# Expert rows gathered in runs of four of one kind instead of in turns, in a one-core encoder layer

## The reference

```python
def _peer(u, w_query, sub_keys, expert_down, expert_up):     # u: 512 tokens x 1024
    ...
        qc = (xc @ w_query).reshape(PEER_CHUNK, PEER_HEADS, 2, PEER_DKEY // 2)
        s_half = jnp.einsum('chpk,pnk->chpn', qc, sub_keys, ...)
        top_s, top_i = lax.top_k(s_half, PEER_TOPK)            # 16 of 128, twice
        ...                                                    # best 16 of the 256 sums
        expert = jnp.take_along_axis(cand_i, best_j, axis=-1)  # of 16384 experts
        g = jax.nn.softmax(best_s, axis=-1)
        u_e = expert_down[expert]                              # one row of 1024 each
        act = jax.nn.gelu(jnp.einsum('chkd,cd->chk', u_e, xc, ...), approximate=False)
        v_e = expert_up[expert]
        return jnp.einsum('chk,chkd->cd', (g * act).astype(xc.dtype), v_e)
```

## Time and profile before

| | us |
|---|---|
| median of 3 runs (1945.47 to 1947.72) | 1947.72 |
| the profiled execution's own time | 1944.45 |
| its span, first to last instruction | 1942.6 |
| PE busy / DVE busy / POOL busy | 1549.1 / 1161.1 / 1002.8 |
| ACT busy | 399.5 |
| mean granted TensorE clock | 0.952 |

### The profile page before, as it was taken

The page is one execution under the profiler, slowest core; times in us unless marked ns, Lnnn a source line. Parts: engine busy times, 40 slices in busy tenths (PEclk is TensorE's granted clock), DMA queues, the critical chain, the costliest instruction groups (busy, mean ns, idle before and its releaser), DMA issues.

```text
span 1942.6 us, 14519 instructions
## 1 busy us (share of the span) xinstructions
PE 1549.1 (80%) x4216; PEld 706.7 (36%) x4216; DVE 1161.1 (60%) x2797; ACT 399.5 (21%) x984; POOL 1002.8 (52%) x1053
## 2 busy tenths in 40 slices
PE   5979999999688779698777879876787877767777
PEld 3434455656333234343223434322233322222223
DVE  6523057749666776576565766676665557666651
ACT  2100045512212212121211211221211211111111
POOL 3000000004566766766666666666666666666663
PEclk8889999999799999899999989999998999999989
DMA  9776242207999999999999999999999999999995
GB/s 321 241 258 194 79 130 44 78 32 229 404 357 374 390 386 366 393 409 370 388 400 350 373 389 407 366 378 367 365 370 373 383 363 351 375 378 377 360 375 226
DMA packets 192772, 620.26 MB, mean 319 GB/s; under 512 B 25695, under 2 KB 26103, under 8 KB 192535
## 3 DMA queue, kind: packets, MB, share of 16 engines
q0 software_dynamic: 147456, 536.94, 72.1%
q1 hardware_dynamic: 45238, 82.41, 12.9%
HBM read 613.12 MB, written 6.16 MB: 319 GB/s over the span
## 4 chain that ended last, share of the span: by engine, by line
PE 29%; POOL 23%; issue 14%; DVE 13%; DMA 12%; another core or an unknown queue 6%; ACT 1%; SPq 1%; DVEq 0%; POOLq 0%; ACTq 0%
POOL big L567 17%; PE pair L577 13%; PE pair L749 13%; POOL region_v L567 5%; DMA big<-in_expert_up,expert_idx 5%; DVE big L1228 4%; DMA big<-in_expert_down,expert_idx 4%; PE pair L613 1%; DMA region_v<-in_expert_up,expert_idx 1%; DMA big<-in_w_in 1%; DMA big<-in_w_ada 1%; DVE region_v L1228 1%; PE pair L701 1%; DVE big L1081 1%
## 5 line engine op out<-in xcount | busy, mean ns | idle before, releaser
L749 PE MATMUL pair<-big 128*128 128x512 f32 x1544 | 764.1, 622 | 206.2 <-DMA big<-in_expert_up,expert_idx 107.1
L1228 DVE CUSTOM_DVE_ANT_0 big<-big,pair 128x1024 f32<-128x1024 f32 x378 | 459.6, 1220 | 304.6 <-DMA big<-in_expert_down,expert_idx 219.7
L749 PEld LDWEIGHTS pair<-big 128*128 128x128 f32 x1544 | 276.0, 194 | 613.1 <-issue 581.9
L567 POOL DMA_INDIRECT big<-in_expert_up,expert_idx x386 | 365.9, 948 | 243.4 <-issue 102.1
L567 POOL DMA_INDIRECT big<-in_expert_down,expert_idx x378 | 360.3, 953 | 118.3 <-issue 108.6
L749 PE MATMUL pair<-region_v,big 128*128 128x512 f32 x504 | 258.3, 636 | 67.2 <-DMA region_v<-in_expert_up,expert_idx 39.1
L577 PE MATMUL pair<-big 128*128 128x512 f32 (+1 forms) x656 | 288.3, 617 | 20.1 <-DMA big<-in_w_in 14.0
L1228 DVE CUSTOM_DVE_ANT_0 region_v<-region_v,pair 128x1024 f32<-128x1024 f32 x134 | 162.9, 1220 | 96.8 <-DMA region_v<-in_expert_down,expert_idx 67.8
L894 ACT ACTIVATE big<-ident,big 128x128 f32<-128x128 f32 x512 | 157.9, 388 | 271.4 <-issue 126.2
L533 POOL TENSOR_SCALAR small<-small 128x4 f32<-128x4 f32 x5 | 1.2, 232 | 356.4 <-DVE small L1106 337.9
L567 POOL DMA_INDIRECT region_v<-in_expert_down,expert_idx x134 | 130.1, 971 | 101.3 <-DVE expert_idx L1166 49.4
(11 more groups left out here) (140 smaller groups left out, 966.0 us busy)
## 6 DMA issues: line engine op xcount, KB each, us to landing
big<-in_w_ada SPq DMA_DIRECT2D x12, 2048.0 KB, 20.7
big<-in_w_query SPq DMA_DIRECT2D x8, 2048.0 KB
big<-in_w_in SPq DMA_DIRECT2D x6, 2048.0 KB, 20.0
big<-na_scr SPq DMA_DIRECT2D x8, 1024.0 KB, 12.2
big<-in_expert_up,expert_idx POOLq DMA_INDIRECT x386
big<-in_expert_down,expert_idx POOLq DMA_INDIRECT x378
big<-in_w_out SPq DMA_DIRECT2D x2, 2048.0 KB, 10.2
region_v<-in_expert_down,expert_idx POOLq DMA_INDIRECT x134
```

Of the source, the lines that this page charges most:

```text
L567: nc.gpsimd.indirect_dma_start(places[place], None, (expert_down if kind == "down" else expert_up)[0], bass.IndirectOffsetOnAxis(expert_id ...
L749: last = nc.tensor.matmul(pair[t % 2][:, s * HALF:(s + 1) * HALF], diag[:, j, :], places[place][:, s * HALF:(s + 1) * HALF], start=(h == 0 ...
L1228: v.tensor_tensor_reduce(out=places[place], in0=places[place], in1=u_cur[:, :], scale=1.0, scalar=0.0, op0=ALU.mult, op1=ALU.add, accum_ou ...
```

## The change

`gather_order()` now goes through the sets in steps of four: four down gathers, then four up gathers, whose sets lie `TOPK + 4 = 20` behind. Nothing else is edited. What PE, DVE and ACT execute, and in which order, stays as it is, except for the numbers of the places that they read and wait for; lines behind 67 move down by one.

```diff
-UP_LAG = TOPK + 3
+RUN = 4
+UP_LAG = TOPK + RUN
...
 def gather_order():
 
     order = []
-    for at in range(SETS + UP_LAG):
-        order += [("down", at)] if at < SETS else []
-        order += [("up", at - UP_LAG)] if at >= UP_LAG else []
+    for at in range(0, SETS + UP_LAG, RUN):
+        order += [("down", at + i) for i in range(RUN) if at < SETS]
+        order += [("up", at - UP_LAG + i) for i in range(RUN) if at >= UP_LAG]
     return order
```

## The result

The changed kernel took 1956.5 us (median of 16 runs, 1944.74 to 1961.0) against 1946.11 us of the kernel before (16 runs, 1941.52 to 1948.62): ratio 1.0043, 95% interval 1.0029 to 1.0057. By the ratio it is slower by 8.4 us. The medians lie 10.4 us apart, because the changed kernel's runs fall into two groups, six from 1944.74 to 1950.78 and ten from 1954.11 to 1961.0. The time forecast was 1954 us, 6 us more than before. Its profiled execution took 1958.89 us, with a span of 1957.1; it lies 14.4 us above the profiled one before, six more than the ratio says, so no single difference between the two traces is taken for the change without an experiment. Of the 14.4 us, 3.6 arise ahead of gather 20 (counted from 0), up to which both kernels issue the same: it went out at 481.66 before and at 485.22 after.

The account below looks back on a forecast made before the run. It took the kernel to be bound by full DMA engines, with 118 us of dips when PE's news reaches POOL late. Terms +6 + 3 - 1 - 4 + 2 = +6 us gave 1954 us; forecast's own range 1946 to 1963, overall 1922 to 1986.

Parts of the forecast that it names:

- What bounds the kernel: Expert stage, 490 to 1914.5 us: DMA engines full at 411 GB/s except dips costing 118 us, when PE's news reaches POOL late.
- The margin, +6: Middle: runs take about 1 us off POOL's margin, pauses 3.5% more frequent, +6 us; bounds 118 us gained, 82 lost.
- The clock, +3: 76 runs without query steps: PE idles 3.3 us, its clock dips, taking margin; +3 us, bounds 0 to +129.
- The head's start, -1: PE's 39 waits for a diagonal, 47.1 us, go, since up set 16h is issued ten gathers behind; -1 us, at most -4.
- The start, -4: Four more gathers, 5.0 us, go out before POOL's first wait, 1 us lost back; -4 us, between -5 and 0.
- DVE's term: Four dots come at once on DVE, but its waits end promptly and the margin stays 8 sets: costed at 0.
- The end, +2: Last down gather 5.0 us earlier, PE works 6.9 us longer on 24 sets, not 20; +2 us, between 0 and +3.
- Sum: Whole kernel: +6 + 3 - 1 - 4 + 2 = +6 us, 1954 us forecast.
- Rival A: POOL's pauses merge in runs, a quarter of 84 waits go: about -23 us, 1925 us; chance 0.27.
- Rival B: Runs without query steps: longer clock dips make POOL pause in most; net about +35 us, 1983 us; chance 0.17.
- Rival C: Nothing measurable: traffic, not order, sets the dips; start and end cancel, 1946 us; chance 0.18.
- What would show it: Signs expected in the profile after: POOL's waits, start wait about 7 us, clock below 0.952, PE's last piece 41.6 us.

Follow-up runs that it names:

- chips B and C: Two chips used for follow-up experiments, where news is late; the kernel before took 1957.42 us on B (33 runs) and 1954.42 us on C (35 runs).
- half the news: Kernel before, but PE raises up_done only behind every second set, by 2: 1956.97 us, ratio 1.0012 (1.0002 to 1.0022).
- chip A: Chip of the first four experiments, where news is prompt; the kernel before took 1849.28 us there (27 runs).
- ten places: Order of the kernel before, but of the 16 places 6 belong to down rows and 10 to up rows: 1956.09 us, ratio 1.0003 (0.9986 to 1.0020).

## Why the prediction was right, point by point

It was right in direction and size, 1954 against 1956.5 us, but three of its terms were sized wrongly, and the errors cancel. The shares below come from ratios with half widths of about 2 us each, some from different chips.

- **What bounds the kernel.** Full DMA engines with dips, and POOL stopped by late news: right on chips B and C and on that of the prediction. It was taken for a property of the kernel and for an effect of the traffic, and it is neither: on A the same kernel has more traffic and prompt news.
- **The margin, +6: wrong.** The step that failed is "one microsecond less in 28 makes the pauses 3.5% more frequent". In runs in the middle alone the whole middle costs 1.0 us (ratio 1.0005), and a margin larger by 5 us wins nothing (1.0003). The waits for PE and "remote" were 170.6 us after, 178 before, both without the start. A wait does not end at a fixed time after the matmul: it ended 12.3 us after it with eight sets and 17.1 with ten.
- **The clock, +3, in the middle: wrong place.** The mean granted clock of the stage did fall to 0.90, as expected, with the idle time between runs as its cause: the in-turns kernel of chip B with runs at the end alone kept 0.95 over the same stretch. But PE has spare time in the middle, and the runs in the middle alone with 0.90 cost 1.0 us (-1.0 to 2.9). The Trainium skill's "TensorE: Matmul & The Clock Gate", section "HAM oscillation — how this bites in real kernels", says that bursts between DMA waits start cold; the traces agree, with 0.90 in runs against 0.95 in turns; a cost shows at the tail alone.
- **The head's start, -1: not to be told apart from 0.** Waits for a diagonal fell from 47.1 us in 39 to 25.1 in 14; they did not go entirely. No ratio moved by it.
- **The start, -4: gained, and lost again.** Counted from gather 20, gather 60 was issued 62.2, 59.6, 59.8 and 59.9 us later in the four traces with runs at the start on chips with late news, and 64.4 to 65.2 in the five with lag 19 or 20 in turns there (half the news left aside): the 4 us are there. But from gather 120 to gather 200 the same four took 122.9, 117.8, 119.0 and 122.6 us, and the five 113.9 to 115.7. There DVE waited for the LayerNorm's deviation, as with runs of eight, 9.4 to 19.3 us at the longest (5.3 to 10.5 in the five), and POOL waited 3.2 to 14.3 us for DVE (5 us at most in the five). This is DVE's term, which the prediction put at 0. The kernel with runs at the start alone is in turns again there and loses the time; the one with runs in the middle alone has runs there and does not (115.2). So it hangs on the start, how is open, and each kernel has one trace. In the ratios, the runs at the start, with lag 20, gave +1.4 us (interval -1.2 to +3.9), and lag 20 in turns +2.0 on chip A: the start itself is about -0.6, give or take 3 us.
- **The end, +2: too small, about +5.** This is the mis-sized term. Lag 20 with runs at the end alone costs 4.9 us (2.7 to 7.0). In the traces, from the last down gather's issue to PE's end were 42.0 us before, and 42.8 to 43.6 in three other kernels that end in turns with lag 19; in the changed kernel's three traces and the one with the end alone they were 52.0, 52.6, 51.3 and 51.4: 8 to 10 us more, where the prediction had 6.9. With lag 20 in turns it was 45.1 us, so 2 to 3 of these 8 to 10 us belong to the lag and the rest to the runs. Four sets more explain the 6.9. The rest, in three of the four traces, is the cold clock behind the idle time in which the last four down rows are transferred (4.39, 4.01 and 3.55 us without work): 18 records in 10.73 us, 2.9 more than at full speed. In the fourth, the changed kernel on B, PE was idle for 2.0 us only and began warm, but stopped for 1.43 us within set 496, for which the profile shows no wait. The other half of the term, the last dot 5.0 us earlier, can't be read off against runs that differ by more than that.
- **Sum.** Middle +1.0, end +4.9, start -0.6: +5.3, give or take 4, against 8.4, 6.9 and 5.1 measured for the whole. The prediction had +8, +2 and -4, again +6. The path that it priced highest, the margin, costs nothing that shows, and the one that costs most, the end, it put at a quarter. That the sum was right is luck: the middle was put too high by 7 us, the end and the start too low by 3 us each.
- **Rival A** (pauses merge): not so; 53 separate pauses of POOL from 520 us on, against 50 before. **Rival B** (cold bursts make POOL pause): the clock fell as it says, but the waits did not rise. **Rival C** held for the middle and for the whole of the rates, and failed at the end.
- **What would show it.** Waits for PE and "remote" at 178 us or more: nearly, 170.6. At up gathers alone: no, 8 of POOL's 74 waits of over 0.31 us were at down gathers, most of them for DVE, 1 of 65 before; nor mostly at the ends of a run (10, 19, 17 and 20 at its four places). Start wait of 7 us: no, 12.0. Clock below 0.952: yes. Last piece of 96 records, 41.6 us: 96 records, 44.22. Waits for DVE after 520 us: 26.6, under the 30 that would have refuted it, but not the 0 that DVE's term said. The kernel with runs in the middle alone has 23.3 us of them and costs 1.0 us (-1.0 to 2.9), so that there they cost nothing that shows.

What stays open: why a chip's news is late; what costs the 3 to 8 us between gathers 120 and 200; whether the changed kernel costs the same on a chip where it is prompt, since it was not run there (the lag, the middle and runs of two cost about 0.1% or less there); and how much of the end is the idle time and how much the cold clock after it.

## What to carry to other kernels

In a stage that a nearly full resource bounds, the order of the requests was worth little in the middle and most at the end, where the work is serial: cost the ends first, and there include what the engine did just before, since an engine left idle can begin its last piece at the lower clock. A margin argument needs a test that widens the margin before it is priced: a wait whose end moves with the margin gives nothing back. When a kernel is slower, find the stretch in which it falls behind before looking at sums over the whole: with runs of eight the long last piece of PE looked like the cause, and the time had been lost 1100 us earlier. And a wait sum of one trace may belong to the chip; compare on the same chip before a mechanism is built on it.

## What the runs showed of the hardware

- The same kernel took 1849.28 us on one chip and 1954 to 1957 on two others (1946 on that of the prediction), steady within 0.6% on each. The difference is the row transfer stage: 408 GB/s against 374 to 377.
- Where it is slow, an engine learns of another's finished work up to 17 us late (22 with ten places for up rows), PE's news to POOL and ACT and, at the start, the landed rows' news to DVE. Where it is fast, `up_done` is there within 0.02 us. It is not the number of transfers under way: by the DMA records, 4 to 14 gathers were in flight on chip A, 8 at the median, and the news was prompt throughout; where it was late, the median was 4. Nor is it the amount of PE's own news or the distance waited for.
- The late news comes in bunches, and mostly when POOL stands still. In the trace of before no raise of `up_done` is recorded from 562.06 to 573.96 us, while POOL issues seven gathers and PE ends sets 23 to 27; POOL stopped at 571.11, and seven raises follow up to 580.57. Over the 49 pauses above 2 us in that trace the first raise comes 3.05 us (median) after POOL's last descriptors, 3.0 to 3.3 us in those of the changed, middle and tail kernels, 3.1 with ten places and 3.7 with half the news. If a wait ends some 3 us after POOL stops, whenever its set was done, a wider margin can't shorten it. That is an inference; it fits the tests of the margin and of the news. At the start of the stage DVE got its news 2.0 us after POOL stopped issuing gathers; that POOL's issuing is what holds the news was not tried.
- At the tail PE had the 1.2 GHz level for its next 1 to 2 sets after 4.39, 4.01 and 3.55 us without work. After about 2 us it went both ways: 2.31 us before set 492 in the trace of before and 2.01 in that of the changed kernel on B left the clock up, 2.12 us before set 491 in the kernel with runs at the start did not.
